# Six conditioning chunks of a streaming layer, computed during the prompt's attention instead of during the input projection

## The reference, cut to what matters

```python
def conditioning(c, w_ada, b_ada):
    mod = jax.nn.silu(c) @ w_ada + b_ada
    return [m[:, None, :] for m in jnp.split(mod, 6, axis=-1)]
...
sh1, sc1, g1, sh2, sc2, g2 = conditioning(c_prompt, w_ada[l], b_ada[l])
...
u = modulate(x, shift, scale)          # layer_norm(x) * (1 + scale) + shift
z = u @ w_in + b_in                    # (384, 1024) @ (1024, 6656)
oa, ob = attend(qa, ka, va, qb, kb, vb)
m = jax.nn.sigmoid(ga) * (oa @ p_a) + jax.nn.sigmoid(gb) * (ob @ p_b)
x = post_norm(x, gate * (m @ w_out), ln_g, ln_b)
# then: router, top 8 of 64 experts, shared expert, gate2, second post_norm
```

## Time and profile before

| | |
|---|---|
| median of 3 runs | 1322.1 us (1322.06 to 1329.15) |
| profiled execution, own time | 1323.07 us |
| its span | 1321.3 us |
| TensorE busy over the span | 1033.8 us (78%) |
| DVE busy | 427.7 us (32%) |
| ACT busy | 239.2 us (18%) |
| DMA, mean | 263 GB/s |

### The profile page before, as it was taken

One profiled execution on the slowest core, in us unless ns is written; L12 is line 12 of the kernel. 1 busy time (PEld: TensorE's weight loads), 2 busy tenths in 40 slices (PEclk: granted clock), 3 DMA queues, 4 the chain that ended last, 5 costly groups with the idle time before them and its releaser, 6 DMA issues.

```text
span 1321.3 us, 23547 instructions
## 1 busy us (share of the span) xinstructions
PE 1033.8 (78%) x8385; PEld 657.7 (50%) x8386; DVE 427.7 (32%) x815; ACT 239.2 (18%) x478; POOL 218.1 (17%) x361
## 2 busy tenths in 40 slices
PE   4899899986576699983787788877877878766865
PEld 3888788875565344542344444444433444433432
DVE  4523324338843113874411111111111121101118
ACT  3222212336455000110110101010100111100100
POOL 0002102000100000201222222222231223212211
PEclk9899999996799799997799889899898998978988
DMA  9587666521063793075689699987999988899955
GB/s 350 173 298 256 223 236 216 184 95 48 1 226 112 274 272 115 32 301 201 215 291 386 229 382 395 370 326 272 408 375 387 328 303 299 308 398 404 396 220 216
DMA packets 97912, 347.52 MB, mean 263 GB/s; under 512 B 15057, under 2 KB 20225, under 8 KB 73146
## 3 DMA queue, kind: packets, MB, share of 16 engines
q1 hardware_dynamic: 81258, 311.56, 63.7%
q0 software_dynamic: 13856, 30.13, 6.9%
q10 hardware_dynamic: 2736, 4.98, 1.0%
HBM read 329.15 MB, written 29.52 MB: 271 GB/s over the span
## 4 chain that ended last, share of the span: by engine, by line
PE 27%; DMA 16%; issue 6%; DVE 2%; SPq 1%; ACT 0%; POOL 0%; POOLq 0%; DVEq 0%; ACTq 0%
PE PS L1771 8%; DMA hT<-h_rows,ixo 7%; DMA W<-w 7%; PE PS L1786 6%; PE PS L1802 4%; PE PS L1827 4%; PE PS L1841 2%; PE PS L1777 1%; DMA vec<-ln_b 1%; PE PS L1759 1%; PE PS L1817 1%; DVE hido L1893 0%; PE PS L1794 0%; DVE hid L1888 0%; DMA W<-expert_rows 0%
## 5 line engine op out<-in xcount | busy, mean ns | idle before, releaser
L1771 PE MATMUL PS<-W,XT 128*32 128x256 f32 x2048 | 130.0, 410 | 48.5 <-DMA W<-w 26.5
L1786 PE MATMUL PS<-W,XTo 128*64 128x256 f32 x1216 | 139.5, 381 | 0.0
L1771 PEld LDWEIGHTS PS<-W,XT 128*32 128x32 f32 x2048 | 80.1, 118 | 114.8 <-issue 90.6
L1786 PEld LDWEIGHTS PS<-W,XTo 128*64 128x64 f32 x1216 | 93.2, 137 | 44.0 <-issue 10.6
L1802 PE MATMUL PS<-W,hidTo 128*64 128x512 f32 x304 | 90.7, 722 | 16.3 <-DVE hidTo L1896 10.7
L431 DVE TENSOR_TENSOR w_lo<-raw,w_hi 128x2048 fp32r<-128x2048 f32 x26 | 59.5, 2288 | 126.1 <-ACT w_hi L371 126.1
L305 PE MATMUL PS<-w_hi,u_hi 128*128 128x512 f32 x240 | 94.4, 393 | 1.7 <-DVE w_lo L431 1.7
L305 PE MATMUL PS<-w_hi,u_lo 128*128 128x512 f32 x240 | 93.5, 389 | 0.0
L305 PE MATMUL PS<-w_lo,u_hi 128*128 128x512 f32 x240 | 93.4, 389 | 0.0
L1827 PE MATMUL PS<-W,hidT 128*32 128x512 f32 x512 | 72.1, 677 | 26.3 <-issue 24.3
L1856 ACT ACTIVATE sg<-PS 64x256 f32<-64x256 f32 x32 | 12.1, 378 | 346.9 <-PE PS L1771 346.9
(11 more groups left out here) (338 smaller groups left out, 1497.8 us busy)
## 6 DMA issues: line engine op xcount, KB each, us to landing
W<-w SPq DMA_DIRECT2D x192, 1024.0 KB, 13.9
raw<-w_in SPq DMA_DIRECT2D x26, 1024.0 KB, 9.2
oaT<-w_ada SPq DMA_DIRECT2D x8, 1536.0 KB, 8.6
W<-expert_rows SPq DMA_DIRECT2D x24, 512.0 KB, 12.5
obT<-w_ada SPq DMA_DIRECT2D x8, 512.0 KB, 8.9
kc<-cache_k_diff SPq DMA_DIRECT2D x8, 512.0 KB, 4.8
vc<-cache_v_diff SPq DMA_DIRECT2D x8, 512.0 KB, 3.5
Wa<-p_a SPq DMA_DIRECT2D x4, 1024.0 KB, 7.5
```

Source lines behind the costliest of these rows:

```text
L1771: mm = pe.matmul(PS[64 * h + 32 * c:64 * h + 32 * c + 32, UP_B + i, 0:F], XT[:, i, k, 32 * c:32 * c + 32], t.W13[:, 2 * i + c, h, k], star ...
L1786: mm = pe.matmul(PS[64 * h:64 * h + 64, XH_B, 0:F], XTo[:, k], t.W13[:, slot, h, k], start=k == 0, stop=k == KD - 1)
```

## The change

The constant MOD_Z = 2 keeps late chunks 0 and 1 where they were. Chunks 2 to 7 (six, called m = 0 to 5 in the new code) go into the attention of the prompt. They get their own buffers: `wada` (two of 2 MB), `b_late`, `mod_late`. Each is now loaded by one transfer of 2 MB and four of the bias. TensorE does a chunk in two halves of 16 matmuls, one half at each step 1 to 12, between scores(n+1) and turn(n-1). DVE adds the bias at steps 3, 5, 7, 9, 11 and after the last step, POOL writes the rows. The first output transposes use PSUM bank 0, since bank 5 now holds the conditioning. `cT`, the transposed conditioning vectors, lives on until the attention ends.

```diff
+MOD_Z, MOD_N = 2, 8
...
-                if c < NA:
+                if c < MOD_Z:
                     load_late_ada(c)
...
-                if c < NA:
+                if c < MOD_Z:
                     pe.wait_ge(ada2_in, 96 * (c + 1))
...
+            def load_late(m):
+                if m >= 2:
+                    sp.wait_ge(late_ev, m - 1)
+                src = t.w_ada[0].rearrange("(k p) n -> p k n", p=P)[:, :, column_of(m):column_of(m) + CW]
+                sp.dma_start(wada[:, m % 2], src).then_inc(late_in[m % 2], 16)
+                for j in range(4):
+                    n0 = column_of(m) + P * j
+                    sp.dma_start(b_q[32 * j:32 * j + 32, m % 2], t.b_ada[:, n0:n0 + P].to_broadcast([32, P])).then_inc(late_in[m % 2], 16)
+
+            load_late(0)
+            load_late(1)
             for b in range(2):
                 load_key_cache(sp, t, b)
+            for m in range(2, len(LATE)):
+                load_late(m)
...
             for tile in range(2):
+                late_rows(range(2) if tile == 0 else range(2, len(LATE)))
                 pool.wait_ge(ms_done, tile + 1)
                 pool.tensor_tensor(ss[:, :], ss[:, :], t.power[:, 0:HA], ALU.pow).then_inc(rms_done, 1)
+            for i in range(2):
+                pool.wait_ge(late_out[i], 64 * len(LATE) // 2)
...
+            def late_part(i):
+                m, h = i // 2, i % 2
+                if h == 0:
+                    pe.wait_ge(late_in[m % 2], 80 * (m // 2 + 1))
+                    if m:
+                        pe.wait_ge(late_ev, m)
+                for k in range(4 * h, 4 * h + 4):
+                    for j in range(4):
+                        mm = pe.matmul(PS[32 * j:32 * j + 32, 5, 0:P], t.cT[:, k], wada[:, m % 2, k, P * j:P * j + P],
+                                       start=k == 0, stop=k == KD - 1)
+                if h:
+                    mm.then_inc(late_mm, 1)
...
                 if n + 1 < len(GR):
                     scores(n + 1)
+                if 0 <= n - 1 < 2 * len(LATE):
+                    late_part(n - 1)
                 if 1 <= n <= len(GR):
                     turn(n - 1)
...
+            def late_rows(m):
+                dve.wait_ge(late_mm, m + 1)
+                if m >= 2:
+                    dve.wait_ge(late_out[m % 2], 64 * (m // 2))
+                dve.tensor_tensor(mod_q[:, m % 2], PS[:, 5, 0:P], b_q[:, m % 2], ALU.add).then_inc(late_ev, 1)
...
                 if n >= 1:
                     weights(n - 1)
+                if n >= 3 and n % 2:
+                    late_rows((n - 3) // 2)
...
+            late_rows(len(LATE) - 1)
             squares(1)
```

More of the change, by code:

```diff
@@ L140, in condition_and_project @@
                 t.obT[:, :, :].rearrange("p k q -> p (k q)")[:, 0:2 * CW].rearrange("p (k n) -> p k n", n=CW))
-        A0, NA = 2 * D // CW, 4 * D // CW
+        A0 = 2 * D // CW
         ada2_in, ada2_mm, ada2_ev = sem("ada2_in"), sem("ada2_mm"), sem("ada2_ev")
@@ L250, in _ @@
             for i in range(2):
-                pool.wait_ge(mod_out[i], 64 * (NA // 2))
+                pool.wait_ge(mod_out[i], 64 * (MOD_Z // 2))
             pool.wait_ge(k_out[0], 96)
@@ L670, in attention_prompt @@
         ms_done, rms_done = sem("ms_done"), sem("rms_done")
+        LATE = list(range(MOD_Z, MOD_N))
+        wada, b_q, mod_q = sb("wada", [P, 2, KD, CW]), sb("b_late", [P, 2, P]), sb("mod_late", [P, 2, P])
+        late_in, late_mm, late_ev = [sem(f"late_in{i}") for i in range(2)], sem("late_mm"), sem("late_ev")
+        late_out = [sem(f"late_out{i}") for i in range(2)]
+        column_of = lambda m: 2 * D + CW * LATE[m]
         block = ctx.enter_context(nc.Block())
@@ L679, in _, with late_rows @@
         def _(sp):
+            def load_late(m):
[8 more added lines that the diff above has]
+            load_late(1)
             for b in range(2):
                 load_key_cache(sp, t, b)
+            for m in range(2, len(LATE)):
+                load_late(m)
         @block.gpsimd
         def _(pool):
+            def late_rows(ms):
+                for m in ms:
+                    pool.wait_ge(late_ev, m + 1)
+                    for j in range(4):
+                        n0 = column_of(m) + P * j
+                        pool.dma_start(t.mod[:, n0:n0 + P], mod_q[32 * j:32 * j + NC, m % 2]).then_inc(late_out[m % 2], 16)
             for tile in range(2):
+                late_rows(range(2) if tile == 0 else range(2, len(LATE)))
                 pool.wait_ge(ms_done, tile + 1)
                 pool.tensor_tensor(ss[:, :], ss[:, :], t.power[:, 0:HA], ALU.pow).then_inc(rms_done, 1)
+            for i in range(2):
+                pool.wait_ge(late_out[i], 64 * len(LATE) // 2)
         nmat = lambda tile, g: (2 if g < 4 else 4) * (tile + 1)
@@ L742, in turn_out @@
                         pe.wait_ge(ot_ev, 3)
+                        pe.wait_ge(late_ev, len(LATE))
                     for m in range(4):
                         src = O[:, tile, P * (4 * b + m):P * (4 * b + m) + P] if b < 2 else OBt[:, tile, P * m:P * m + P]
-                        mm = pe.transpose(PS[:, 5 + n * tile, P * m:P * m + P], src, t.ident[:, :])
+                        mm = pe.transpose(PS[:, 5 + n if tile else 0, P * m:P * m + P], src, t.ident[:, :])
                     mm.then_inc(ot_mm, 1)
@@ L830, in out_turned @@
                     dst = t.oaT[:, 4 * b:4 * b + 4] if b < 2 else t.obT[:, :]
-                    act.copy(dst[:, :, P * tile:P * tile + P], PS[:, 5 + n * tile].rearrange("p (k q) -> p k q", k=4)).then_inc(ot_ev, 1)
+                    act.copy(dst[:, :, P * tile:P * tile + P], PS[:, 5 + n if tile else 0].rearrange("p (k q) -> p k q", k=4)).then_inc(ot_ev, 1)
             for n in range(len(GR) + 2):
@@ L2073, in streaming_layer @@
                 t.join = scoped(attention, "join", [P, 64])
+                t.cT = scoped(attention, "cT", [P, KD, 32])
                 with ExitStack() as scope:
@@ L2077, in streaming_layer @@
                     t.u_lo = scoped(scope, "u_lo", [P, NT, KD, P], F32R)
-                    t.cT = scoped(scope, "cT", [P, KD, 32])
                     t.w_hi, t.w_lo = scoped(scope, "w_hi", [P, 2, 4, CW], F32R), scoped(scope, "w_lo", [P, 2, 4, CW], F32R)
```

## The result

Over 17 runs of each, the changed kernel takes **1312.7 us** (median; 1306.64 to 1318.9) and the kernel before 1322.8 us. The ratio is **0.9917**, with a 95% interval from 0.9899 to 0.9934: 11.0 us less by that ratio, with 8.7 to 13.4 as the interval (the two medians lie 10.1 us apart). The forecast was 1310.6 us, and 11.5 us less. A later comparison gave 0.9941 (0.9916 to 0.9966), 7.8 us less. In the profiles shown here the two sides that make the net are each about 3 us larger than forecast, and the errors cancel; the projection's side is known to about 3 us only (experiment 3).

What follows compares the result with a forecast made beforehand. The prediction took TensorE to bound the projection and the attention's end, DVE the attention between. The projection's 17.0 us less the attention's 5.5 us gave 11.5 us saved, 1322.1 becoming 1310.6 us, range 1304 to 1317.

Steps and rivals of the forecast that it cites:

- What the projection gives back: Projection: removing late chunks 2 to 7 from TensorE's list saves their matmuls and waits, 17.0 us, lower bound 11.5.
- (a): Start of the prompt's attention: TensorE waits for the first 2 MB load, delaying DVE by 2.8 us (1 to 6).
- (b): Prompt's attention: the third load waits for an emptied buffer and comes some 1 us late, costing 0.5 us (0 to 3).
- (c): Attention loop: five bias additions of 0.28 us on DVE, the engine that sets the pace, cost 1.4 us.
- (d): Attention, step 6: with TensorE at the upper clock level, DVE's 0.74 us wait for slow scores goes, -0.7 us.
- (e): Attention's tail: the last two halves stand ahead of turns where TensorE sets the end, costing 1.5 us (0 to 4.1).
- The upper level holds through the attention: Rival: TensorE keeps its upper clock level in the prompt's attention, giving 1307.7 us; chance 0.15.
- The lower level stays: Rival: TensorE stays at its lower clock level in the attention, giving 1321.3 us, no gain; chance 0.10.
- The projection doesn't give the waits back: Rival: the projection returns only 11.5 us, giving 1316.1 us; chance 0.07.
- Slower, because loads are late at each chunk: Rival: attention loads land late at each chunk, losing from 12.3 us landing time on, 1331 us at 14; chance 0.05.
- My own sign for being wrong: Waits for `wada` at over two chunks, DVE waiting for scores in most steps, or projection shortened under 15 us.
- the other signs: Projection's end about 277 us, first-half wait about 4, turn(0) 10.5 in, scores 1.1, streams' attention 11 to 12 earlier.

Runs made afterwards that it cites:

- experiment 3: The changed kernel, but all eight late chunks also stay in the projection, so six are computed in both places; one run, 1327.8 us.
- Experiment 4: The kernel before the change, with SP issuing the next w_in halves ahead of the late chunk's 2 MB; one run, 1317.5 us.
- experiment 1: The changed kernel, with the bias transfers on a semaphore of their own, so TensorE's halves wait for the weights alone; one run, 1311.6 us.
- experiment 8: The changed kernel, with the moved chunks taking turns between PSUM banks and the loads left as they were; one run, 1309.3 us.
- experiment 6: The changed kernel, with the first moved chunk loaded during the projection into oaT and obT, bias on its own semaphore; six runs, 1305.7 us, ratio 0.9882.
- experiment 7: As experiment 6, with the moved chunks also going to PSUM banks 5, 3, 5, 3, 5, 1 instead of always 5; six runs, 1304.3 us, ratio 0.9861.
- Experiment 9: The changed kernel, with DVE's bias addition of each moved chunk done twice, once into a spare tile; one run, 1314.0 us.
- the repeat: The changed kernel measured once more without an edit, in a later comparison; twelve runs, 1313.7 us, ratio 0.9941 to the kernel before.
- experiment 2: The changed kernel, with each chunk's four bias transfers issued ahead of its 2 MB of weights; one run, 1316.0 us.

## Why the forecast held, term by term

**What the projection gives back: 17.0 forecast, 20.0 measured.** The mechanism held at every chunk. Counted from the start of the chunk's last product to the next chunk's first, chunks 2 to 7 gave back 2.82, 2.35, 2.39, 6.09, 2.40 and 1.98 us against 2.81, 2.10, 2.10, 6.08, 1.97 and 1.97: 18.0 instead of 17.0. The difference is at chunks 3, 4 and 6, where I had read only the late matmuls and their wait, or had taken chunk 7's price. The slow products after the wait of chunk 5, which I named and left out at half a microsecond, gave 1.1. Of the 1.66 us that the projection's last chunks had waited for `w_lo`, 0.67 is left. Against that, what stands ahead of late chunk 2 runs 0.8 us later. What is left, 0.6 us, I can't place. All this is read from one pair of profiles; against the projection of experiment 3 the sum is 16.9, so that the 3 us over the forecast are within what two profiles of the same list differ by. Experiment 4 shows the cause of the largest term: the wait of the earlier trace rows goes when the weights are put ahead in the queue.

**(a) First load: 2.8 forecast, 3.2 measured.** I had the half start 8.5 us into the block. It started at 9.92, because the four bias transfers count on the same semaphore and land behind the 2 MB (experiment 1: 8.22 without them). I had not counted the bias transfers in that wait, though every DMA of a moved step has to count. The weights alone took 8.3 us where the rows gave 8.4. By the rule of the Trainium skill, "DMA: Bandwidth & Descriptors", section on the two cost components, the estimate would have been 6.8 us; the shortest of the six landings is 7.4 us, so here the rule is too low. The further 0.9 us that I expected in the step behind it did not come: steps 3 and 4 kept their 3.68 us.

**(b) Third load: 0.5 forecast, 4.0 measured. This is the term that was mis-sized**, by more than its upper bound of 3. That the load waits until DVE has emptied the first chunk, and that 7.4 us are then left, was right: it is issued at 295.64, and the half would have to start at 302.9 for logits(7) to be in time, 7.2 us later. I get that point from experiment 8: there the half starts 2.2 us after logits(6) (303.30, 301.10) and logits(7) come 1.46 us later than 3.97 us behind logits(6), the distance before; so a half at the upper level may start 0.74 us after logits(6) begin, which are at 302.14 here. Three things went wrong behind that. From issue to half it took 9.7 us and not 8.4 (+1.3; by experiment 1 the bias pieces are 0.7 of it, the rest is open). I let TensorE's slack take half of the lateness, though the 7.4 us already held it (+0.5, and 0.2 for 7.2 instead of 7.4). And the wait cost the clock: from the half's start to logits(7), the same instructions took 3.2 us in experiment 8 at the upper level and 4.8 here (+1.6). So DVE is late by 2.4 us for the load and 1.6 for the clock. Experiment 1 splits the same way: 1.8 and 2.7 (5.9 us at the lower level), 4.4 together. The windows from the half's start to logits(7) show the granted clock, 0.64 with the change, 1.00 in experiment 8 and 0.50 in experiment 1, for the same 52 records:

```profile
305.30:310.10 4.80, 4.80 (x52) 3.75 (x56) 0.71 (x5) 1.99 (x7) 0.00 (x0) 0.64 0.97 363
...
303.30:306.53 3.23, 3.23 (x52) 2.53 (x56) 1.58 (x8) 1.52 (x5) 0.22 (x1) 1.00 1.01 381
...
302.20:308.09 5.89, 5.89 (x52) 4.37 (x56) 1.26 (x7) 2.60 (x9) 0.00 (x0) 0.50 0.86 323
```

Experiments 6 and 7 test the point of 0.74 us: without its wait of 1.83 us the half of experiment 7 would start 1.76 us ahead of that point, so it is 0.07 us late, and the step to logits(7) takes 4.04 us, 0.07 over 3.97. In experiment 6 the wait of 1.26 us stays inside the slack, and the step takes 3.96 us.

The Trainium skill, "TensorE: Matmul & The Clock Gate", section Part 1, says that activity releases the clock; scores at 0.72 us from 293.75 on agree, and the durations behind the long waits show the other direction.

**(c) Additions: 1.4 forecast, 0.0 measured.** Between DVE's last update of `A` and the next logits lay 0.47 us in the kernel before, though the update takes 0.35. The addition depends on neither and runs between them: 295.06 to 295.53 is 0.47 us again. Experiment 9 shows that the gap holds one such addition and not a second.

**(d) Scores at step 6: -0.7 forecast, -0.6 measured**, by the clock, as argued.

**(e) Tail: 1.5 forecast, 1.6 measured** in the first profile, and 3.6 in the repeat, 3.4 in experiment 6, 1.4 in experiment 7. The bounds (0 to 4.1) were right, and the value is known to about 1.4 to 3.6. I had counted the sixth addition at its own 0.28 us; in fact DVE waits 3.79 us ahead of it for the last half. What the tail is short of is TensorE, not DVE.

**The sum.** The projection gave 3.0 us more, the attention took 2.7 us more (8.2 against 5.5, with (a) +0.4, (b) +3.5, (c) -1.4, (d) +0.1, (e) +0.1). Had the projection only kept its 17.0, the forecast would have been 3 us too low. That the total agreed to half a microsecond is luck. The attention's side is the sure one: its block is 8.2 and 9.7 us longer in the two profiles of the change, against 5.5. Of the projection's side only 17 to 20 us is known.

**The rivals.** *The upper level holds through the attention*: no; the level comes up at step 4 and is lost again behind each longer wait (mean 0.80 up to 341.6 us, 0.93 in the tail, against 0.73 and 0.80). *The lower level stays*: no. *The projection doesn't give the waits back*: no, it gave back more. *Slower, because loads are late at each chunk*: its mechanism acted, at two chunks of six. The turning point that it gave, 12.3 us, was not reached; the two loads took 10.0 and 9.7 us from issue to half. (By its own terms the point is 12.1 us: the sum leaves out 0.3 us for each of the last two chunks.) My own sign for being wrong, waits for `wada` at more than two chunks, was not met, but only just: there were two. Of the other signs, the last product came at 273.8 us and not at 277, the first half waited 5.9 us and not 4, turn(0) came 11.8 us into the block and not 10.5, and the scores' level and the start of the streams' attention were as written.

The time outside these two stages can't carry an argument of this size. From the memset to the end of the program the code is the same in every version; it took 952.3 us before, 947.8 with the change, 956.8 in its repeat, and between 950.8 and 960.1 in the others. That is why single executions were read by the length of stages, and why experiment 6, whose profiled execution has one of the longest rests, is judged by its six runs.

## What to carry to other kernels

Moving transfers into a stage where the DMA is idle does not make them free. With two buffers, a load is issued when the first buffer is emptied and is wanted when the second one is used up, so compare that interval with the time from issue to use, the small transfers on the same semaphore included, and add to a long wait what TensorE's clock can lose in it. One more place for a chunk, filled in the stage before, took away the whole delay in the loop here and left that of the tail. And before work is moved because of the waits around it, try the order in the queue: here 2 to 5 us of what the projection gave back came from two kinds of entries that had stood the wrong way round.

## What the runs showed of the hardware

- **Small transfers behind a large one.** Four loads of `b_late` (32x128 each) landed in 7.0 us (median) when they stood behind a load of 2 MB on the same queue, and in 2.0 us ahead of it (experiment 2). Their four issues took 2.4 to 4.1 us behind the block's first 2 MB, and 2.3 us (experiment 2) to 3.3 us (experiment 7) with nothing ahead of them in the block; later in the block they took 2.0 us and more right behind a load, and 1.7 us ahead of it (experiment 2). So a block's first issues are slow with and without a load ahead.
- **A free slot on DVE.** An independent 128x128 addition between two dependent instructions added 0.00 us to the step; a second one added 0.20 us, less than its 0.28.
- **The clock after a wait.** In the nine profiles with chunks in the attention, the 32 records of a half took 1.08 us (the upper level) behind each wait of up to 1.89 us, and 1.93 or 1.94 us (the lower) behind each of 4.19 us or more. Between them both came up: 1.08 us behind waits of 3.22 and 3.96 us, 1.93 or 1.94 behind 1.92, 2.34 and 3.47. Some halves without a wait of their own took 1.93 us as well (318.75 us in experiment 1, 322.11 in experiment 9), so the last wait alone does not tell the level. A wait of some microseconds on TensorE can cost more than its length: up to 2.7 us in the instructions behind it.
